# Sixteen gate tiles of the even layer turned by VectorE, with taps, layer norm, attention rows and the order of products rearranged

## The reference, cut to what matters

```python
def even_layer(h, ...):
    p = rms_norm(h, norm_g) @ w_in          # 2048 -> 9232 channels
    qkv_a, z_a, b_a, a_a, glu_b, z_b, q_m, z_m = jnp.split(p, cuts, axis=-1)
    # A: gated DeltaNet, 8 heads of 128, chunks of 64 rows
    o_a = rms_norm(gated_delta_rule(q, k, v, beta, g), dn_norm_g) * silu(z_a)
    # B: convolution module, 1024 channels, 31 taps
    c = causal_depthwise_conv(glu_b[..., :CV] * sigmoid(glu_b[..., CV:]), dw_w) + dw_b
    o_b = silu(layer_norm(c, ln_g, ln_b)) * silu(z_b)
    # M: cross-attention into the memory, 4 heads of 256
    o_m = softmax(rms_norm(q_m) @ mem_k.T * s) @ mem_v * silu(z_m)
    return concatenate([o_a, o_b, o_m], -1) @ w_out

def odd_layer(h, ...):
    p = rms_norm(h, norm_g) @ w_in          # 2048 -> 10240 channels
    q_c, k_c, v_c, z_c, q_m, z_m = jnp.split(p, cuts, axis=-1)
    # C: stick-breaking attention, 16 heads of 128
    o_c = stick_breaking_attention(rms_norm(q), rms_norm(k), v) * silu(z_c)
    o_m = ...                               # M as above, with its own q_m, z_m
    return concatenate([o_c, o_m], -1) @ w_out

mkv = rms_norm(mem, mem_norm_g) @ w_mem_kv  # keys and values of the memory, once
h = x; h = h + even_layer(h, ...); h = h + odd_layer(h, ...)
```

## Time and profile before

| | |
|---|---|
| Time, median of 3 runs | 1356.57 us (1355.96 to 1357.27) |
| The profiled execution | 1356.2 us, span 1354.5 us |
| PE, busy share of the span | 99% (1337.6 us) |
| DVE | 72% (973.3 us) |
| ACT | 56% (751.8 us) |
| POOL | 8% (104.3 us) |
| Read from HBM | 234.32 MB, 176 GB/s over the span |
| Granted clock, mean | 0.997 of full speed |

### The profile page before, as it was taken

The page is one execution under the profiler, slowest core; times in us unless marked ns, Lnnn a source line. Parts: engine busy times, 40 slices in busy tenths (PEclk is TensorE's granted clock), DMA queues, the critical chain, the costliest instruction groups (busy, mean ns, idle before and its releaser), DMA issues.

```text
span 1354.5 us, 18214 instructions
## 1 busy us (share of the span) xinstructions
PE 1337.6 (99%) x6813; PEld 1134.0 (84%) x6813; DVE 973.3 (72%) x1498; ACT 751.8 (56%) x1201; POOL 104.3 (8%) x104
## 2 busy tenths in 40 slices
PE   9999999999999999999999999999999999998998
PEld 9998899888888888888888888888888888877887
DVE  5557688898998987745656487686787786685663
ACT  6556623475346567664446447756666657644341
POOL 2000300003100000000002020010200200000000
PEclk9999999999999999999999999999999999998999
DMA  9655554555646755654555665574565555643652
GB/s 313 196 185 172 153 179 140 157 189 146 198 140 198 269 177 172 210 170 141 164 164 185 201 188 151 163 218 153 191 182 157 188 173 167 198 144 109 201 187 78
DMA packets 134512, 239.31 MB, mean 177 GB/s; under 512 B 13936, under 2 KB 19993, under 8 KB 134425
## 3 DMA queue, kind: packets, MB, share of 16 engines
q1 hardware_dynamic: 131705, 233.43, 54.9%
q10 hardware_dynamic: 2720, 4.72, 1.1%
HBM read 234.32 MB, written 3.80 MB: 176 GB/s over the span
## 4 chain that ended last, share of the span: by engine, by line
PE 72%; DVE 7%; issue 1%; ACT 1%; POOL 0%; ACTq 0%; DVEq 0%; POOLq 0%
PE job L1700 22%; PE job L1702 21%; PE job L1701 21%; DVE wlo L1283 2%; PE mixer L1752 2%; DVE mix L1595 1%; DVE cvr L1531 1%; PE mixer L1992 1%; PE mixer L1972 1%; PE mixer L2014 1%; PE mixer L2001 1%; PE mixer L1861 0%; DVE scr L1663 0%; PE mixer L2000 0%; PE mixer L2015 0%
## 5 line engine op out<-in xcount | busy, mean ns | idle before, releaser
L1700 PE MATMUL job<-whi,xhi 128*128 128x512 f32 x1536 | 615.5, 401 | 0.0
L1702 PE MATMUL job<-whi,xlo 128*128 128x512 f32 x1536 | 599.9, 391 | 0.0
L1701 PE MATMUL job<-wlo,xhi 128*128 128x512 f32 x1536 | 598.7, 390 | 0.0
L1283 DVE TENSOR_TENSOR wlo<-raw,whi 128x1024 fp32r<-128x1024 f32 x431 | 524.7, 1237 | 87.6 <-ACT whi L933 86.7
L933 ACT ACTIVATE whi<-raw 128x1024 fp32r<-128x1024 f32 x431 | 446.6, 1055 | 178.2 <-PE job L1702 133.6
L1702 PEld LDWEIGHTS job<-whi,xlo 128*128 128x128 f32 x1536 | 288.6, 188 | 62.1
L1701 PEld LDWEIGHTS job<-wlo,xhi 128*128 128x128 f32 x1536 | 289.2, 188 | 56.7
L1700 PEld LDWEIGHTS job<-whi,xhi 128*128 128x128 f32 x1536 | 288.9, 188 | 56.6
L1706 PE MATMUL job<-xhi,whi 128*128 128x256 f32 x376 | 108.4, 288 | 0.0
L1708 PE MATMUL job<-xhi,wlo 128*128 128x256 f32 x376 | 106.4, 283 | 0.0
L1707 PE MATMUL job<-xlo,whi 128*128 128x256 f32 x376 | 106.3, 283 | 0.0
(11 more groups left out here) (282 smaller groups left out, 1005.4 us busy)
## 6 DMA issues: line engine op xcount, KB each, us to landing
raw<-in_od_w_in_dram SPq DMA_DIRECT2D x160, 512.0 KB, 4.0
raw<-in_ev_w_in_dram SPq DMA_DIRECT2D x143, 512.0 KB, 4.0
raw<-in_ev_w_out_dram SPq DMA_DIRECT2D x48, 512.0 KB, 4.8
raw<-in_od_w_out_dram SPq DMA_DIRECT2D x48, 512.0 KB, 4.5
raw<-in_w_mem_kv_dram SPq DMA_DIRECT2D x32, 512.0 KB, 4.5
reg<-in_mem_dram ACTq DMA_DIRECT2D x4, 512.0 KB, 4.9
hid<-in_x_dram ACTq DMA_DIRECT2D x4, 512.0 KB, 7.9
hid<-in_x_dram SPq DMA_DIRECT2D x3, 512.0 KB, 8.8
```

The source lines that it names most:

```text
L1283: vec.tensor_tensor(wlo[:, c % RING, :, :], raw[:, c % RAWS, :, :], whi[:, c % RING, :, :].bitcast(F32), ALU.subtract).then_inc(s_lo, 1)
L1700: mm(out_, xh, hi, start=first, stop=False)
L1701: mm(out_, xh, lo, start=False, stop=False)
L1702: return mm(out_, xl, hi, start=False, stop=last)
```

## The change

- **Even layer's gates.** The sixteen tiles 0 to 15 are turned by VectorE (zb) as the others were; TensorE's transposes and ScalarE's copies of them go. zb 0 to 7 stand at positions 116 to 123, zT0 to zT7 at 119 to 126; zb 8 to 11 at 138 to 141, zT8 to zT11 at 141 to 144; zb 12 to 15 at 146 to 149, zT12 to zT15 at 149 to 152. The waits for a free place in `mix` (`s_t`, `s_ow`) move from ScalarE to VectorE's first zb of a group.
- **Taps and layer norm.** The planner now counts 0.2 of a chunk for a zb, and with that the taps run up to position 159; lnm is at 161, lnr at 171, lno7 at 182.
- **Heads of the odd layer.** The four sbT of a group take one position instead of two; of each group's first head the output (sbo) comes one position later.
- **Memory gates of the odd layer.** Tiles 32 to 39 go the other way: TensorE transposes them (zT at 379 to 382 and 386 to 389), ScalarE copies them.
- **Order of products.** A chunk's products with the high weights (eight) come first, ahead of which TensorE waits for ScalarE's `s_hi`; then it waits for VectorE's `s_lo` and makes the four with the remainder. Before, it waited for `s_lo` first, and the three products of a tile stood together. The last chunk is unchanged.

```diff
--- before.py
+++ after.py
@@ -136,7 +136,7 @@
 CONV_SHARE = 0.31
 
 
-VECTOR_SHARE = {"evac": .5, "dnC": 1.3, "dnU": .5, "dnV": .35, "dnR": .25, "dnG": .4, "inF": 2.7, "inT": .55, "d4y": .4, "d5c": .15,
+VECTOR_SHARE = {"evac": .5, "zb": .2, "dnC": 1.3, "dnU": .5, "dnV": .35, "dnR": .25, "dnG": .4, "inF": 2.7, "inT": .55, "d4y": .4, "d5c": .15,
                 "d5e": .1, "d6": .25, "gate": .25, "za": .45, "glu": .45, "zT": .16, "xt": .18, "mf": .16, "bas": .1}
 TENSOR_SHARE = {"dnB": .26, "dnG": .55, "d4x": .32, "d4y": .45, "d5a": .08, "d5b": .16, "d5c": .16, "d5d": .08,
                 "d5e": .08, "d7": .08, "gT": .08, "zT": .08, "xt": .08}
@@ -238,9 +238,15 @@
 
     for g in range(2):
         stream(2, after(J_GLU[g] + 1) + 6 * g, [(("glu", g), 2 + g)] + [(("gT", ct), 1) for ct in range(4 * g, 4 * g + 4)])
-    stream(3, max(after(J_ZB + 1), int(inverted) + 1), [(("zT", n), 1) for n in range(8)])
-    q = stream(3, max(after(J_ZM), oa), [(("zT", n), 1) for n in range(8, 12)])
-    stream(3, max(after(J_ZM + 1), q), [(("zT", n), 1) for n in range(12, 16)])
+    def gates(m, at):
+        stream(3, at, [(("zb", 4 * m + a), 1) for a in range(4)])
+        return stream(3, at + 3, [(("zT", 4 * m + a), 1) for a in range(4)])
+
+    gates(0, max(after(J_ZB), int(inverted) + 1))
+    gates(1, max(after(J_ZB + 1), int(inverted) + 5))
+    q = max(after(J_ZM), oa) + 4
+    gates(2, max(after(J_ZM) - 1, oa))
+    gates(3, max(after(J_ZM + 1) - 1, oa + 4))
     for j in range(len(JOBS)):
         late = 5 if j == J_GLU[1] + 1 else 0 if J_OM <= j < J_ODIN or j == len(JOBS) - 1 else 1 if j else 3
         stream(-1, CH0[j + 1] + late, [(("evac", j), 0)])
@@ -293,18 +299,16 @@
     stream(6, CH0[J_ODIN] + 4, [(("sbk", 0), 0)])
     p = 0
     for g in range(4):
-        s = [(("sbn", g), 5)] + [(("sbB", 8 * g + i), 1) for i in range(8)] + [(("sbT", h), .5) for h in range(4 * g, 4 * g + 4)]
+        s = [(("sbn", g), 5)] + [(("sbB", 8 * g + i), 1) for i in range(8)] + [(("sbT", h), .25) for h in range(4 * g, 4 * g + 4)]
         s += [("at", after(J_ODIN + 4 * g + 3)), (("tab", g), 0)]
         for h in range(4 * g, 4 * g + 4):
-            s += [(("sbz", h), 2), (("sbe", h), 1), (("zT", 16 + h), 0), (("sbc", h), 1), (("sbo", h), 0)]
+            s += [(("sbz", h), 2), (("sbe", h), 1), (("zT", 16 + h), 0), (("sbc", h), 1 if h % 4 else 2), (("sbo", h), 0)]
         p = stream(6, max(p, after(J_ODIN + 4 * g + 1)), s)
-        stream(5, after(J_ODIN + 4 * g + 3) - 1, [(("zb", 4 * g + i), 1) for i in range(4)])
-    last_head = p
+        stream(5, after(J_ODIN + 4 * g + 3) - 1, [(("zb", 16 + 4 * g + i), 1) for i in range(4)])
     p = stream(6, max(p + 1, after(J_ODIN + 17)), [(("mqs", 2), 1.5), (("mqs", 3), 1.5)]
                + [(("mqT", dt), .5) for dt in range(8, 16)])
-    for m, at in ((4, after(J_ODIN + 18) - 1), (5, max(after(J_ODIN + 19) - 1, int(last_head) + 1))):
-        stream(4, at, [(("zb", 4 * m + i), 1) for i in range(4)])
-        stream(4, at + 3, [(("zT", 16 + 4 * m + i), 1) for i in range(4)])
+    stream(4, after(J_ODIN + 18), [(("zT", n), 1) for n in range(32, 36)])
+    stream(4, after(J_ODIN + 19) - 1, [(("zT", n), 1) for n in range(36, 40)])
     p = stream(6, max(p, after(J_ODIN + 19)), attend(4))
 
     plan = []
@@ -1148,12 +1152,11 @@
             def do_zT(n):
                 kt = zsource(n)[3]
                 sc.wait_ge(s_zp, n + 1)
-                if n < 8:
-                    sc.wait_ge(s_t[0], 2 * LEVELS + 2)
-                    sc.wait_ge(s_t[1], 2 * LEVELS + 2)
-                elif n < 16:
-                    sc.wait_ge(s_ow, 16)
-                if n < 16:
+                if n == 32:
+                    sc.wait_ge(s_xl, F_H)
+                elif n == 37:
+                    sc.wait_ge(s_sbW, 16)
+                if n >= 32:
                     act(mix[:, kt, :], M[3][:, 0:S], ACT.Copy)
                     act(M[3][:, S:2 * S], M[3][:, 0:S], ACT.Tanh, scale=0.5).then_inc(s_zc, 1)
                     return
@@ -1583,12 +1586,12 @@
 
             def do_zb(i):
                 m, a = divmod(i, 4)
-                j, slot, _, kt = zsource(16 + 4 * m)
+                j, slot, _, kt = zsource(4 * m)
                 if a == 0:
                     ve.wait_ge(*evac_done(j))
-                    ve.wait_ge(s_xl, F_OM if m < 4 else F_H)
-                    if m == 5:
-                        ve.wait_ge(s_sbW, 16)
+                    for q in (((s_t[0], 2 * LEVELS + 2), (s_t[1], 2 * LEVELS + 2)) if m < 2 else ((s_ow, 16),) if m < 4
+                              else ((s_xl, F_OM),)):
+                        ve.wait_ge(*q)
                 src = proj[32 * a:32 * a + 32, slot, :, :].rearrange("p t (h n) -> p h t n", h=4)
                 for b in range(4):
                     dst = mix[32 * b:32 * b + 32, kt:kt + 4, :].rearrange("p h (t n) -> p h t n", t=T)
@@ -1700,12 +1703,6 @@
                 mm(out_, xh, hi, start=first, stop=False)
                 mm(out_, xh, lo, start=False, stop=False)
                 return mm(out_, xl, hi, start=False, stop=last)
-
-            def three_turned(out_, k, n, hi, lo, first, last):
-                cols = slice(128 * n, 128 * n + 128)
-                mm(out_, hi[:, cols], xhi[:, k, :], start=first and n % 2 == 0, stop=False, skip_group_check=True)
-                mm(out_, hi[:, cols], xlo[:, k, :], start=False, stop=False, skip_group_check=True)
-                return mm(out_, lo[:, cols], xhi[:, k, :], start=False, stop=last, skip_group_check=True)
 
             def do_open(i):
                 pe.wait_ge(*((s_hi0, 1), (s_xl, 2), (s_lo, 1))[i])
@@ -1729,24 +1726,37 @@
                     pe.wait_ge(*evac_done(j - 2))
                 if all(JOBS[q][4] != fill for q in range(j)):
                     pe.wait_ge(s_xl, fill + 2 * i + 2)
+                if c < NCH - 1:
+                    pe.wait_ge(s_hi, c)
+                    by_channel = j in CHANNEL
+                    for k in (2 * i, 2 * i + 1):
+                        h, s = whi[:, c % RING, k % 2, :], SLOT[fill + k]
+                        for n in range(4 if by_channel else T):
+                            cols = slice(128 * n, 128 * n + 128)
+                            for x, first in ((xhi, k == 0), (xlo, False)):
+                                if by_channel:
+                                    mm(pj[j % 2][n // 2][:, S * (n % 2):S * (n % 2) + S], h[:, cols], x[:, s, :],
+                                       start=first and n % 2 == 0, stop=False, skip_group_check=True)
+                                else:
+                                    mm(pj[j % 2][n][:, :], x[:, s, cols], h, start=first, stop=False)
+                    pe.wait_ge(s_lo, c + 1)
+                    for k in (2 * i, 2 * i + 1):
+                        l, s = wlo[:, c % RING, k % 2, :], SLOT[fill + k]
+                        for n in range(4 if by_channel else T):
+                            cols = slice(128 * n, 128 * n + 128)
+                            if by_channel:
+                                ins = mm(pj[j % 2][n // 2][:, S * (n % 2):S * (n % 2) + S], l[:, cols], xhi[:, s, :],
+                                         start=False, stop=k == kts - 1, skip_group_check=True)
+                            else:
+                                ins = mm(pj[j % 2][n][:, :], xhi[:, s, cols], l, start=False, stop=k == kts - 1)
+                    ins.then_inc(s_pe, 1)
+                    return
                 pe.wait_ge(s_lo, c + 1)
-                if c == NCH - 1:
-                    for t in range(T):
-                        for k in (2 * i, 2 * i + 1):
-                            ins = three(pj[j % 2][t][:, :], SLOT[fill + k], t, whi[:, c % RING, k % 2, :],
-                                        wlo[:, c % RING, k % 2, :], k == 0, k == kts - 1)
-                        ins.then_inc(s_pe, 1)
-                    return
-                for k in (2 * i, 2 * i + 1):
-                    if j in CHANNEL:
-                        for n in range(4):
-                            ins = three_turned(pj[j % 2][n // 2][:, S * (n % 2):S * (n % 2) + S], SLOT[fill + k], n,
-                                               whi[:, c % RING, k % 2, :], wlo[:, c % RING, k % 2, :], k == 0, k == kts - 1)
-                        continue
-                    for t in range(T):
+                for t in range(T):
+                    for k in (2 * i, 2 * i + 1):
                         ins = three(pj[j % 2][t][:, :], SLOT[fill + k], t, whi[:, c % RING, k % 2, :],
                                     wlo[:, c % RING, k % 2, :], k == 0, k == kts - 1)
-                ins.then_inc(s_pe, 1)
+                    ins.then_inc(s_pe, 1)
 
             def turn(dst, src):
                 return nc.tensor.transpose(dst, src, ident[:, :])
@@ -1935,7 +1945,7 @@
                 ins.then_inc(s_lvp, 1)
 
             def do_zT(n):
-                if n >= 16:
+                if n < 32:
                     return
```

## The result

The changed kernel takes 1358.86 us (median of 20 runs, 1357.84 to 1360.01) against 1356.43 for the kernel before (20 runs alternating with it). The ratio is 1.0015, 95% interval 1.0008 to 1.0022: a small loss, 2.4 us by the medians. The profiled execution took 1358.6, with a span of 1356.5 us against 1354.5, 2.0 more.

The account below looks back on a forecast made before the run. TensorE, busy 99%, was taken as the bound, so time changes by its instructions and by waits where VectorE is late. 1356.2 + 11 - 3.3 - 7.2 = 1356.7 us profiled, 1357.1 as a median; 8-in-10 range 1349 to 1364.

Parts of the forecast that it names:

- Part 1: Even layer's sixteen gate tiles turned by VectorE instead of TensorE: +11 us for the even layer, bounds +5 and +15.
- VectorE's queue up to the remainders of chunk 144: Even layer from position 116: VectorE's work ahead of that date grows by 14.1 us by list, 14.6 position by position.
- After chunk 144: Rest of even layer: transposes saved -1.0, L1127's wait gone -0.6, more VectorE steps before the memory fill +1.4 us.
- the rival of the clock: Even layer: clock falls at chunk 144's wait, half rate for 4 us costs 2.4; 1358 to 1361 us, chance 0.13.
- Part 2: Even layer's taps and layer norm later: same VectorE time elsewhere, 0 us, bounds 0 and +1.
- Part 3: Order of products in each chunk, high parts first: remainders never late, 0 us, bounds -2 and +2.
- Part 4: Odd layer's heads: first output of each group one chunk later covers four waits of 0.82 us; -3.3, bounds -3.3 and -1.
- Part 5: Odd layer's memory gates, eight tiles back to TensorE: waits and lowered clock go, -7.2 us net, bounds -8 and 0.
- What was to show it: Signs: waits on L1484 near 405 to 425 us, 5 to 6 at chunk 144 near 489, VectorE over 95%, chunks 386-397 about 47.

Follow-up runs that it names:

- the kernel with no turned tile: Changed kernel with the even layer's sixteen gate tiles back on TensorE and ScalarE, taps and layer norm at their old positions: 1345.78 us, ratio 0.9925.
- the run with the last eight tiles: Changed kernel with gate tiles 0 to 7 given back to TensorE, VectorE turning only 8 to 15 of the even layer: 1350.63 us.
- the kernel with TensorE kept busy: Changed kernel with 24 useless products of 512 columns put ahead of TensorE's wait at chunk 144: 1358.62 us.

## Why the prediction came out as it did

The forecast was 1357.1 us; measured 1358.9. The shape was right in every part, a loss in the even layer and a gain in the odd one that nearly cancel, and the sizes were off by 2 us in all. By the chunk starts the errors are 1.6 us too little loss in part 1, 0.7 and -0.2 too little gain in parts 4 and 5, and 0.4 us of scatter: that they partly cancel is luck.

- **Part 1** was forecast at +11; the run without it gives 12.6 by the chunk starts, 13.1 by the medians. The waits came where I had put them: 8.4 us at positions 120 to 125 (I had about 9), 5.9 at chunk 144 (I had about 6). The term that was too small is VectorE's queue up to the remainders of chunk 144: +14.6 in the forecast (14.1 by its list), 15.5 measured (392.21 to 491.0, 98.8 us, against 391.63 to 474.9, 83.3). By the two timelines: the turned steps took 21.8 (forecast 21.5), the seven tap steps that left gave 4.7 (5.4: 0.67 us each, not 0.765), the gate products 0.5 (0.7), the idle time used up 2.6 (2.6), and the waits for ScalarE's tanh were four, 1.65 us together (three, 1.3). Three of these four:

```profile
409.98 0.42 DVE L1605 SCALAR_TENSOR_TENSOR mix<-mixer,mix 128x256 f32<-128x256 f32 x1 [0.46 <-ACT mixer L1165]
430.71 0.42 DVE L1605 SCALAR_TENSOR_TENSOR mix<-mixer,mix 128x256 f32<-128x256 f32 x1 [0.45 <-ACT mixer L1165]
436.45 0.42 DVE L1605 SCALAR_TENSOR_TENSOR mix<-mixer,mix 128x256 f32<-128x256 f32 x1 [0.29 <-ACT mixer L1165]
```

  That VectorE's idle time is 9.7 us both times is a coincidence of that sum: 2.6 us of it were used up, and the tanh waits and 0.9 us of small gaps around the stream transposes came. Of the old waits 7 us came back (three of 1.0 before L1487, 2.2 and 1.8 for GpSimd), and the forecast had left those standing. A further 0.45 us at chunk 144 is no part of the loss: the kernel with no turned tile starts that chunk 0.45 us later than the kernel before, and against it the changed kernel is 12.25 us late there, not 12.7.
- **After chunk 144** I had +1.4 for a wait at the memory fill. In its place stands the fall of the clock, 1.87; with the clock kept up the wait comes, 1.63 us. So the term was right in kind and size, and the rival of the clock happened beside it at no price: its "half rate for 4 us costs 2.4" should have been 2.0 (half of 4), 1.87 was measured, and next to nothing of it reached the end. The saved transposes and L1127's wait came to -1.56, forecast -1.6.
- **Part 2** was set at nothing. In the changed kernel's trace no wait belongs to it, but no run undoes it alone. And the reason was incomplete: I named ScalarE's and the readers' margins and left GpSimd's sums out. They cost 2.9 us (3.7 by the chunk starts) in the run with the last eight tiles, where the layer norm stands at 156; with the layer norm three positions later they cost nothing.
- **Part 3** was set at 0; the old order gives 1358.45 against 1358.86.
- **Part 4** was -3.3, the chunk starts show -3.95, undoing it costs 3.7. (The positions 259 to 263, given for the third head group, are those of the first; the third has 323 to 327 in the plan. No sum uses them.)
- **Part 5** was -7.2; the chunk starts show -7.0, undoing it costs 6.8. The eleven chunks were to take about 47 us and take 46.6.
- 0.4 us is lost ahead of chunk 112, where no part but the order of products acts. It is scatter between executions: chunk 112 starts between 377.5 and 378.0 us in twelve of the thirteen traces (the other is the one with 3.4 us lost near 190 us), and the kernel with TensorE kept busy, the same as the changed one up to there, starts it at 377.51, as the kernel before does.
- **What was to show it:** all did, but for VectorE's busy share, which I put over 95% up to chunk 144. It was 90% (89.68 of 99.4): my own list left it 8.4 us of idle time (9.7 - 2.6 + 1.3) in 98, which is 91%, so the 95% did not fit the sum. Chunk 144 started at 491.1, not near 489.

The rule that the prediction weighed (the Trainium skill, "VectorE: DVE Perf Modes", Rules for kernel authors: a 128x128 transpose on TensorE if PSUM will do) was borne out for the tiles beside the DeltaNet steps (the eight cost 11.5 us, 7.8 of it up to chunk 126) and not for tiles 8 to 15: with the taps moved away, turning those on VectorE gained 2.4 to 3.4 us (1343.42 and 1342.38 against 1345.78). Up to chunk 144 TensorE was the engine short of time: in the kernel with no turned tile it is busy 86.64 of 87.20 us there (391.7 to 478.9), VectorE 77.60.

## What to carry to other kernels

When work is moved from the engine that is full to one that is not, what counts is what is queued between it and the next date at which the full engine needs an answer: eight turned tiles that begin beside the steps that two engines hand to each other cost 11.5 us, and eight others gained 3.4 us some twenty positions later once movable work had been shifted away. A planner that is told far too little of a step's cost leaves movable work in the way: a turned step takes 0.65 of a chunk, and for the last eight tiles the shares 0.2, 0.4 and 0.5 gave 1350.63 (1347.72 with the layer norm alone moved), 1343.42 and 1342.38 us; 0.65 itself was not run. And changes that are tried together should be timed apart: here 10.7 us of gain lay under 12.6 to 13.1 us of loss.

## What the hardware showed that I had not expected

- The clock did not follow from the length of one wait. The wait of 2.7 us near 427 us is there in the changed kernel and in the one with part 5 undone, which has the same work and the same waits up to that point. The clock stayed up in the first and fell in the second:

```profile
426.00:431.00 5.00, 3.24 (x14) 2.40 (x14) 3.46 (x10) 1.65 (x7) 0.00 (x0) 1.00 0.37 105
426.00:431.00 5.00, 3.54 (x11) 2.93 (x12) 3.46 (x10) 1.94 (x7) 0.00 (x0) 0.66 0.34 105
```

  The wait of 3.1 us at chunk 144 likewise lowered the clock in one kernel (0.66 over 480 to 485 us) and not in another with the same work up to there (1.00). A wait of 2.0 us was followed by 0.67 over 5 us. The longest, 5.9 us, brought the 1.2 GHz level in each of the four traces that have such a wait at chunk 144 (5.8 to 5.9 us).
- A clock that falls can cost nothing, where another engine sets the next date: chunk 144 took 1.87 us longer, and a wait of 1.63 us for VectorE went in return. The same happened near 427 us: with the clock down there, a wait of 0.9 us that the changed kernel has at 432 is gone, and chunk 126 starts at 434.90 against 434.95.
